# mLSTM core: value products with the tokens on the partitions, a column of ones, statistics as columns, a ring of seven weight tiles

## What is computed

```python
inter = bt + m[..., None]
mt = jnp.maximum(inter, dmat.max(-1))
w_inter = jnp.exp(inter - mt)
sqk = jnp.einsum('bhtd,bhsd->bhts', qt, kt) * jnp.exp(dmat - mt[..., None])
num = (w_inter[..., None] * jnp.einsum('bhtk,bhkv->bhtv', qt, c_mat)
       + jnp.einsum('bhts,bhsv->bhtv', sqk, vt))
den = w_inter * jnp.einsum('bhtk,bhk->bht', qt, n_vec) + sqk.sum(-1)
ht = num / jnp.maximum(jnp.abs(den), jnp.exp(-mt))[..., None]
...
h = h_fwd + h_bwd
```

## Time and profile before

| | us |
|---|---|
| median of 3 runs | 4366.0 |
| lowest, highest | 4365.65, 4366.83 |
| the profiled execution, its own time | 4371.4 |
| span of its trace | 4369.6 |
| PE busy in the span | 3929.4 (90%) |
| DVE busy | 2095.5 (48%) |
| ACT busy | 1521.8 (35%) |

### The profile page before, as it was taken

One profiled execution on the slowest core, in us unless ns is written; L12 is line 12 of the kernel. 1 busy time (PEld: TensorE's weight loads), 2 busy tenths in 40 slices (PEclk: granted clock), 3 DMA queues, 4 the chain that ended last, 5 costly groups with the idle time before them and its releaser, 6 DMA issues. The chain is left out here.

```text
span 4369.6 us, 51714 instructions
## 1 busy us (share of the span) xinstructions
PE 3929.4 (90%) x20400; PEld 2995.5 (69%) x20400; DVE 2095.5 (48%) x3118; ACT 1521.8 (35%) x2347; POOL 400.0 (9%) x354
## 2 busy tenths in 40 slices
PE   7888778879999998889789999999988799999998
PEld 5456667668878776566567878876656577777876
DVE  4867464574343335536546443333544635543332
ACT  4444312533332224314444332233313534333232
POOL 0024322000011112010000001100000000001100
PEclk9899778979999998889999999999989999999999
DMA  3011001203322222011112322222101022332222
GB/s 109 10 51 44 1 2 51 67 10 112 93 86 96 84 86 66 29 44 43 67 48 82 95 91 92 95 80 79 49 29 58 1 102 74 93 94 87 94 79 73
DMA packets 83486, 289.30 MB, mean 66 GB/s; under 512 B 9168, under 2 KB 9296, under 8 KB 82000
## 3 DMA queue, kind: packets, MB, share of 16 engines
q1 hardware_dynamic: 83136, 286.30, 20.4%
q10 hardware_dynamic: 144, 0.15, 0.0%
HBM read 284.32 MB, written 2.10 MB: 66 GB/s over the span
## 5 line engine op out<-in xcount | busy, mean ns | idle before, releaser
L547 DVE TENSOR_TENSOR weights_lo_r<-raw_weights,weights_hi_r 128x1024 fp32r<-128x1024 f32 (+2 forms) x554 | 633.1, 1143 | 1752.3 <-ACT weights_hi_r L541 1752.2
L541 ACT ACTIVATE weights_hi_r<-raw_weights 128x1024 fp32r<-128x1024 f32 (+2 forms) x554 | 547.5, 988 | 1865.2 <-PE ps L614 1829.4
L613 PE MATMUL ps<-xn_r,weights_hi_r 128*128 128x512 f32 x2816 | 1117.2, 397 | 0.0
L612 PE MATMUL ps<-xn_hi,weights_hi_r 128*128 128x512 f32 x1952 | 805.1, 412 | 84.4 <-DVE xn_r L607 27.1
L614 PE MATMUL ps<-xn_hi,weights_lo_r 128*128 128x512 f32 x1952 | 777.9, 399 | 0.0
L613 PEld LDWEIGHTS ps<-xn_r,weights_hi_r 128*128 128x128 f32 x2816 | 539.9, 192 | 126.9 <-issue 10.6
L612 PEld LDWEIGHTS ps<-xn_hi,weights_hi_r 128*128 128x128 f32 x1952 | 377.2, 193 | 203.7 <-issue 93.8
L614 PEld LDWEIGHTS ps<-xn_hi,weights_lo_r 128*128 128x128 f32 x1952 | 376.7, 193 | 83.0
L612 PE MATMUL ps<-y_r,weights_hi_r 128*128 128x512 f32 x1056 | 421.3, 399 | 1.6 <-PEq L858 1.6
L614 PE MATMUL ps<-y_r,weights_lo_r 128*128 128x512 f32 x1056 | 421.0, 399 | 0.0
L612 PE MATMUL ps<-hidden_hi,weights_hi_r 128*128 128x512 f32 x528 | 215.9, 409 | 31.9 <-DVE hidden_r L607 31.9
(11 more groups left out here) (490 smaller groups left out, 5521.2 us busy)
## 6 DMA issues: line engine op xcount, KB each, us to landing
raw_weights<-in_w_ffn_dram SPq DMA_DIRECT2D x132, 512.0 KB, 3.7
raw_weights<-in_w_down_dram SPq DMA_DIRECT2D x48, 512.0 KB, 3.5
raw_weights<-in_w_out_dram SPq DMA_DIRECT2D x24, 512.0 KB, 3.5
bias_table<-in_window_bias_dram SPq DMA_DIRECT2D x8, 1280.0 KB, 10.5
raw_weights<-in_w_down_dram SPq DMA_DIRECT2D x24, 384.0 KB, 3.1
raw_weights<-in_w_hgrn_dram SPq DMA_DIRECT2D x16, 512.0 KB, 3.4
raw_weights<-in_w_mix_ssm_dram SPq DMA_DIRECT2D x16, 512.0 KB, 3.7
raw_weights<-in_w_a_qk_dram SPq DMA_DIRECT2D x16, 512.0 KB, 3.5
```

Source lines behind the costliest of these rows:

```text
L541: act.activation(self.k.w_hi[:, g % 2, 0:chunk.width], self.k.raw[:, slot, 0:chunk.width], ACT.Copy)\
L547: dve.tensor_tensor(self.k.w_lo[:, g % 2, 0:chunk.width], self.k.raw[:, slot, 0:chunk.width], self.k.w_hi[:, g % 2, 0:chunk.width].bitcast ...
L612: pe.matmul(out, w_hi, x_hi, start=start, stop=False)
L613: pe.matmul(out, w_hi, x_lo, start=False, stop=False)
```

## The change

Only the core block and what prepares it change.

- **Value products turned round.** `dist` blocks of 128 keys x 128 queries become the stationary operand, and the moving operand is the v tile with the tokens on the partitions and a 129th column of ones (`v_one`, 128 x 4 x 4 x 129; GpSimd sets the ones). One product of 129 columns gives the values and, in the last column, the sum of weights, with queries on the partitions. A step has 4, 3, 2 or 1 such products, a unit 10. The all-ones product is gone.
- **Statistics as columns.** The preparation transposes the m rows too (8 more small transposes), ACT takes exp(-m) of a 128x32 tile (`floor_cols`), and the spread of the floor row is gone. `finish` does the maxima and the reciprocal on 128x4 tiles. The forward unit's values are scaled by ACT in 4 activations of 128x128 (`scale_first`) into `tap`; the backward unit's are scaled and added by DVE in 4 instructions of 128x128.
- **Turning back.** PE transposes the head's sum (4 transposes of 128x128, `turn`) into bank 6, and ACT copies it to `y` (`take`).
- **Ring of seven, one step later.** `dist` has 7 buffers, and the weights overwrite it, so `prob` is gone. PE calls `weigh(s - 2)` and DVE `weight(s - 2)`; `finish` moves behind the fourth step of a unit. Before its bound, DVE waits only that the ring's buffer is free. The spread into bank u % 2 waits for the bounds of the unit two before, no longer for its end.

The diff, cut to its core:

```diff
@@ project @@
-            width = tokens[1].shape[2]
+            width = int(np.prod(tokens[1].shape[2:]))
...
-                    act.activation(tokens[1][:, j, :], k.ps[:, (t0 + j) % 4, 0:width], ACT.Copy).then_inc(tokens_used, 1)
+                    o, taken = tokens[1][:, j], k.ps[:, (t0 + j) % 4, 0:width]
+                    if len(o.shape) == 3:
+                        taken = taken.rearrange("p (h v) -> p h v", h=o.shape[1])
+                    act.activation(o, taken, ACT.Copy).then_inc(tokens_used, 1)
...
@@ MlstmPreparation @@
+        pool.memset(self.one_col, 1.0).then_inc(self.edges, 1)
...
-                mm = pe.transpose(self.cols[:, j, r, :], self.g_[:, r, j * P:(j + 1) * P],
-                                  k.const("ident", H)[:, 0:H])
+                for to, rows in ((self.cols, self.g_), (self.m_cols, self.m_)):
+                    mm = pe.transpose(to[:, j, r, :], rows[:, r, j * P:(j + 1) * P], k.const("ident", H)[:, 0:H])
...
-        act.wait_ge(self.rows_ready, 10)
-        act.activation(m_[:, :, :], m_[:, :, :], ACT.Exp, scale=-1.0).then_inc(self.m_ready, 1)
         act.wait_ge(self.cols_turned, 1)
+        act.activation(self.m_col[:, :, :, :], self.m_cols, ACT.Exp, scale=-1.0).then_inc(self.m_ready, 1)
         act.activation(self.g_col[:, :, :, :], self.cols, ACT.Copy).then_inc(self.cols_ready, 1)
...
@@ mlstm_branch @@
-        v_tok = sb("v_tok", [P, NT, A_WIDTH])
+        v_one = sb("v_tok", [P, NT, H, P + 1])
...
+            RING = 7
+            dist = raw[:, :, :].rearrange("p a b -> p (a b)")[:, 0:RING * T].rearrange("p (a t) -> p a t", a=RING)
...
+            def values(u, i):
+                return k.ps[:, 4 + 2 * (u % 2) + i // 2, (i % 2) * (P + 1):(i % 2) * (P + 1) + P + 1]
             @block.tensor
             def _(pe):
...
                     u, back, h, j, ts = place(s)
                     pe.wait_ge(prob_ready, s + 1)
                     if s % NT == 0 and u >= 2:
-                        pe.wait_ge(h_ready, u - 1)
-                    pr = prob[:, s % 2, ts]
-                    pe.matmul(k.ps[:, 4 + u % 2, ts], v_tok[:, j, h * P:(h + 1) * P], pr, start=(s % NT == 0),
-                              stop=(s % NT == NT - 1))
-                    pe.matmul(k.ps[:, 6 + u % 2, ts], k.const("ones"), pr, start=(s % NT == 0),
-                              stop=(s % NT == NT - 1)).then_inc(pv_done, 1)
-                    if s % NT == NT - 1:
-                        pe.wait_ge(bounded, s + 1)
-                        pe.matmul(bank(k.ps, u % 2), k.const("ident", H)[:, h:h + 1].broadcast_to([H, P]),
-                                  m_[:, back, :], start=True, stop=True).then_inc(floor_spread, 1)
+                        if back:
+                            pe.wait_ge(y_ready, h)
+                        else:
+                            pe.wait_ge(first_half, NT * h)
+                    for i in range(0, j + 1) if back else range(j, NT):
+                        mm = pe.matmul(values(u, i), dist[:, s % RING, i * P:(i + 1) * P], v_one[:, j, h, :],
+                                       start=(s % NT == 0 and i % 2 == 0), stop=(j == (0 if back else i)),
+                                       skip_group_check=True)
+                    mm.then_inc(pv_done, 1)
+                def turn(h):
+                    pe.wait_ge(both_halves, NT * (h + 1))
+                    for i in range(NT):
+                        mm = pe.transpose(k.ps[:, 6, i * P:(i + 1) * P], tap[:, h % 2, i * P:(i + 1) * P],
+                                          k.const("ident"))
+                    mm.then_inc(turned, 1)
                 for s in range(STEPS):
                     u, back, h, j, ts = place(s)
                     if s % NT == 0:
                         if u >= 2:
-                            pe.wait_ge(h_ready, u - 1)
+                            pe.wait_ge(bounded, NT * (u - 1))
                         pe.matmul(bank(k.ps, u % 2), k.const("ident", H)[:, h:h + 1].broadcast_to([H, P]),
                                   M_[:, back, :], start=True, stop=True).then_inc(spread, 1)
                     if s >= 2:
                         pe.wait_ge(prob_ready, s - 1)
                     pe.matmul(k.ps[:, 2 + s % 2, ts], qk[:, H + h, j * P:(j + 1) * P], qk[:, h, ts],
                               start=True, stop=True).then_inc(qk_done, 1)
-                    if s:
-                        weigh(s - 1)
+                    if s >= 2:
+                        weigh(s - 2)
+                    if s % NT == 0 and u >= 3 and back:
+                        turn(h - 1)
+                weigh(STEPS - 2)
                 weigh(STEPS - 1)
+                turn(H - 1)
             @block.gpsimd
             def _(pool):
                 for s in range(STEPS):
                     u, back, h, j, ts = place(s)
                     pool.wait_ge(exped, s + 1)
-                    d = dist[:, s % 2, j * P:(j + 1) * P]
+                    d = dist[:, s % RING, j * P:(j + 1) * P]
                     pool.tensor_tensor(d, d, k.const("ge" if back else "le"), ALU.mult).then_inc(masked, 1)
             @block.scalar
             def _(act):
-                def absolute(u):
-                    act.wait_ge(pv_done, NT * (u + 1))
-                    act.activation(den[:, u % 2, :], bank(k.ps, 6 + u % 2), ACT.Abs).then_inc(den_ready, 1)
+                def scale_first(u):
+                    h = u // 2
+                    act.wait_ge(scale_step, 3 * u + 3)
+                    if h >= 2:
+                        act.wait_ge(turned, h - 1)
+                    for i in range(NT):
+                        act.activation(tap[:, h % 2, i * P:(i + 1) * P], values(u, i)[:, 0:P], ACT.Copy,
+                                       scale=stat[:, u % 2, i:i + 1]).then_inc(first_half, 1)
+                def take(h):
+                    act.wait_ge(turned, h + 1)
+                    act.activation(y[:, h, :], bank(k.ps, 6), ACT.Copy).then_inc(y_ready, 1)
                 for s in range(STEPS):
                     u, back, h, j, ts = place(s)
                     act.wait_ge(bounded, s + 1)
-                    act.activation(dist[:, s % 2, ts], dist[:, s % 2, ts], ACT.Exp, scale=-1.0).then_inc(exped, 1)
-                    if s % NT == 2 and u:
-                        absolute(u - 1)
-                absolute(UNITS - 1)
+                    act.activation(dist[:, s % RING, ts], dist[:, s % RING, ts], ACT.Exp, scale=-1.0).then_inc(exped, 1)
+                    if s % NT == 3 and u and back:
+                        scale_first(u - 1)
+                    if s % NT == 0 and u >= 3 and back:
+                        take(h - 1)
+                take(H - 1)
             @block.vector
             def _(dve):
                 def weight(s):
                     u, back, h, j, ts = place(s)
+                    d = dist[:, s % RING, ts]
                     dve.wait_ge(masked, s + 1)
                     dve.wait_ge(qk_done, s + 1)
-                    if s >= 2:
-                        dve.wait_ge(pv_done, s - 1)
-                    dve.tensor_tensor(prob[:, s % 2, ts], dist[:, s % 2, ts], k.ps[:, 2 + s % 2, ts], ALU.mult)\
-                        .then_inc(prob_ready, 1)
+                    dve.tensor_tensor(d, d, k.ps[:, 2 + s % 2, ts], ALU.mult).then_inc(prob_ready, 1)
                 def finish(u):
-                    back, h, d = u % 2, u // 2, den[:, u % 2, :]
-                    dve.wait_ge(den_ready, u + 1)
-                    dve.wait_ge(floor_spread, u + 1)
-                    dve.tensor_tensor(d, d, bank(k.ps, u % 2), ALU.max).then_inc(den_step, 1)
-                    dve.wait_ge(den_step, 3 * u + 1)
-                    dve.reciprocal(d, d).then_inc(den_step, 1)
-                    dve.wait_ge(den_step, 3 * u + 2)
+                    back, h, r = u % 2, u // 2, stat[:, u % 2, :]
+                    sums = k.ps[:, 4 + 2 * (u % 2):6 + 2 * (u % 2), P:2 * P + 2:P + 1]
+                    pairs = lambda ap: ap.rearrange("p (a b) -> p a b", a=2)
+                    dve.wait_ge(pv_done, NT * (u + 1))
+                    dve.scalar_tensor_tensor(out=pairs(r), in0=sums, scalar=-1.0, in1=pairs(m_col[:, :, back, h]),
+                                             op0=ALU.mult, op1=ALU.max).then_inc(scale_step, 1)
+                    dve.wait_ge(scale_step, 3 * u + 1)
+                    dve.tensor_tensor(pairs(r), sums, pairs(r), ALU.max).then_inc(scale_step, 1)
+                    dve.wait_ge(scale_step, 3 * u + 2)
+                    dve.reciprocal(r, r).then_inc(scale_step, 1)
                     if back:
-                        dve.tensor_tensor(d, d, bank(k.ps, 4 + u % 2), ALU.mult).then_inc(den_step, 1)
-                        dve.wait_ge(den_step, 3 * u + 3)
-                        dve.tensor_tensor(y[:, h, :], y[:, h, :], d, ALU.add).then_inc(h_ready, 1)
-                    else:
```

(54 more changed lines are left out.)

2 lines of the change are left out of this document (1 added, 1 removed).

## The result

| | median us | lowest to highest | runs |
|---|---|---|---|
| before | 4365.8 | 4360.3 to 4366.8 | 4 |
| changed | 4269.6 | 4268.3 to 4270.8 | 4 |

The ratio is 0.9779, 95% interval 0.9766 to 0.9792: 96 us less. The forecast was 4266.6. The profiled execution of the changed kernel takes 4268.3, against 4371.4 before: 103.1 less.

The account below looks back on a forecast made before the run. The core was taken as a PE-DVE loop at two buffers' lead, PE paying for its gaps in clock. Gains of 107.3 - 6 - 1.9 = 99.4 us took 4371.4 to 4272.0, less 5.4 for the median: 4266.6, range 4240 to 4300.

Parts of the forecast that it names:

- The sum: Whole kernel: 107.3 gained in the cores, minus 6 for clock and 1.9 for transposes, gives 99.4 us less.
- Plain boundary 6.9 us, turning boundary 7.6: Core, between units: four boundaries of 6.9 us with PE idling 1.2 before q.k, three of 7.6 where a head turns back.
- the turning chain: Where a head is turned back: `take` waits for transposes, then second step's exp, mask and weight follow; P at 7.6 us.
- Value products at 0.118 us with their loads hidden: PE in the core: 20 instructions a unit step at 0.118 us at the full clock, 2.36 us in all.
- Rival 3: Value products' weight loads stand bare, adding 3.8 us a unit, 61 in all: 4328; chance 0.05.
- The small operations at 0.18 us each, the four scalings at 1.1: DVE's `finish`: three 128x4 operations, together 0.54 us, and the backward unit's four 128x128 instructions, 1.1 in all.
- Start 6.6, end 4.9 us: Core's ends: 6.6 us until unit 0's fourth q.k product, 4.9 from the last such product to the end of `take`.
- Clock: Core: one more halved stretch of 7 us a layer, costing 3 us each, 6 in all; mean clock 0.9 or more.
- Restart of the next projection: Behind the core: PE's gap shrinks from 5.95 to about 3 us; gain left at nought, range 0 to 4 us.
- Rival 1: Core is PE-bound with a shorter boundary wait, a unit costing PE's 5.9 us: 4242; chance 0.12.
- Rivals 4 and 5: Slower through exposed value products, 4464, chance 0.04; no measurable change because the gain returns behind the core, chance 0.02.
- Rival 2: Clock stays down for half of the core, 14.6 us more a layer instead of 3: 4290; chance 0.18.

Follow-up runs that it names:

- third version: Changed kernel with DVE's weight ahead of the bound at a unit's start, spread before the fourth q.k product, `take` one step later: 4233.1 us, again 4236.0.

## Why the prediction was right, step by step

- **The sum, and some luck.** On the profiled execution the forecast was 4272.0 and 4268.3 was measured, 3.7 lower: the cores gained 102.9 us where 107.3 - 6 = 101.3 were laid out, and the 1.9 us for the eight more transposes a layer don't show (the changed profile is 0.9 and 0.5 us longer ahead of the two cores and 1.6 shorter behind them, less than such stretches differ between profiles of one kernel). For the median the forecast then took off 5.4 us, because the profile before lay that far above its median; the profile of the changed kernel lies 1.3 us below its median. The two misses, 3.7 and 6.7 us, have opposite signs and leave the 3 us between 4266.6 and 4269.6. That closeness is luck; the layout of the cores is not.
- **Plain boundary 6.9 us, turning boundary 7.6.** Measured 6.88 and 7.61. The wait of 1.2 us in front of q.k is 1.17, released by DVE's weight, and the turning chain (transposes L2942, `take` L2986, exp, mask, weight) shows as laid out; POOL's mask releases the weight, and that the fourth q.k product:

```profile
1811.76 0.60 PE L2942 MATMUL ps<-consts,tap 128*128 128x128 f32 x4
...
1812.39 0.60 ACT L2986 ACTIVATE y<-ps 128x512 f32<-128x512 f32 x1 [1.76 <-PE ps L2942]
...
1812.89 1.02 ACT L2991 ACTIVATE qk_raw<-qk_raw 128x384 f32<-128x384 f32 x3
...
1813.97 0.56 DVE L3005 TENSOR_TENSOR qk_raw<-qk_raw,ps 128x384 f32<-128x384 f32 x1 [1.44 <-POOL qk_raw L2971]
...
1814.58 0.49 PE L2955 MATMUL ps<-qk 128*128 128x128 f32 x2
```

- **Value products at 0.118 us with their loads hidden.** Measured 0.11. Rival 3, bare loads, is out. The Trainium skill, page "TensorE: Matmul & The Clock Gate", Part 3, Packing small matmuls, has the rule by which a load overlaps running matmuls only in other row groups; loads of all 128 rows overlap here, so the trace does not bear it out. The same part also lets a load go ahead into a background weight buffer. With that the measured step agrees, though no run shows the buffer itself.
- **The small operations at 0.18 us each, the four scalings at 1.1.** Measured 0.19, 0.19, 0.22 from start to start, and 1.13; ACT's four take 1.14, 0.29 each and just under the 0.3 to 0.58 laid out. All lie beside PE's work.
- **Start 6.6, end 4.9 us.** The fourth q.k product starts 5.6 us after the first spread in the first core and 7.1 in the second, 6.4 in the mean (the first spread takes 1.30 and 1.47 us, against 2.04 in the earlier trace rows, so the clock rose earlier), and in the first core, from the last fourth q.k product, 1845.23, to the end of `take` at 1850.18 pass 4.95.
- **Clock.** One halved stretch of 7 us a core, at a price of 3 us, was allowed on top of the slow start. Behind the first unit the first core has one unit with a halved piece (8.55 us for 6.88, a price of 1.7), the second two (8.57 and 8.54, 3.4 in all). With the start, at a mean of 0.94 the first core spent 12% of 62.8 us, 7.5, on the lower level, the second at 0.89 22%, 14.5; the 0.9 or more that the prediction wanted to see was just missed there. Cores of 64.9 us were forecast, 62.5 and 65.8 measured (without the 0.3 us to the next block).
- **Restart of the next projection.** It begins halved as before, although PE now idles 0.94 us in front of it and not 5.95. The prediction put that gap at about 3 us; leaving the gain at nought was right:

```profile
1850.48 0.77 PE L612 MATMUL ps<-xn_hi,weights_hi_r 128*128 128x512 f32 x1 [0.94 <-PEq L2899]
...
1851.05 0.63 PE L613 MATMUL ps<-xn_r,weights_hi_r 128*128 128x512 f32 x1
```

- **What the prediction did not see.** It counted PE's saved columns and DVE's saved stall into one layout and never asked what either is worth alone. The runs did: the stall alone is worth 36 us a core, the all-ones products alone nothing or a little less than nothing, and the last 12 to 14 us come only with the rest of the change, the longer lead among it. The ring's depth stood in the text only as cover, the order at the boundary as a wait to be taken as it is; they turned out to be worth 50 to 55 and 7 to 14 us a core.
- **Rival 1** (PE-bound, 4242) is out for this kernel: the wait stands. Its reading of the cause was right, though. With the order changed at both places (third version) PE is busy without a gap, a unit costs 5.64 or 6.08 us, near the 5.9 counted for PE's work, and the kernel takes 4233 to 4236.
- **Rivals 4 and 5** (slower, or the gain returns behind the core) are out: the step is 0.11 us, and 102.9 of the 103.1 us are gained in the cores.
- **Rival 2** (clock down for half of the core) is out for this kernel, but it is the mechanism of every run that was slower than laid out: the ring of three, the reciprocal put back, the all-ones products left out.

## What to carry to other kernels

Where PE waits for another engine in a loop, shorten the other engine's longest instruction first, and give the loop one more step of lead. Here, taking work off PE while that wait stood only made PE idle longer and lowered its clock. Lay one period of the loop end to end from rows of the trace and look for an instruction that stands behind one whose input comes late: moving it in front of that one cost nothing here and gave 7 and 9 us of blocks of 63 and 66 us. Before sizing a ring, ask which engine's step each wait points to: one buffer too few turned overlap into taking turns.

## What the runs showed of the hardware

- Removing 64 of 224 PE instructions from a core left PE as long busy as before (95.15 against 93.42 us), because the mean granted clock fell from 0.81 to 0.62.
- With waits of about 1 us in front of every step (ring of three, units of 13 to 16 us, so 3 to 4 us a step) the clock was at the lower level for most of the core (a mean of 0.63). With one wait of 1.17 us in 6.9 us the mean was 0.89 to 0.94, and nearly without waits 0.92 to 0.98. The share of waiting alone doesn't order these: with every q.k product doubled the same 1.16 us stood in 9.03 us, and twice as many units (10 of 14) fell below the full clock.
- A float32 product of 128 or 129 columns with a 128-column load of its own costs 0.11 to 0.12 us an instruction at the full clock, next to the 0.11 that 128 columns of a 512-column product take (0.86 us in two instructions). So the load costs next to nothing beside it.
- The same code ahead of the first core took between 1772 and 1788 us in the profiles of the changed kernel and its variants. The same kernel alone differs: 1787.7 and 1780.3 for the changed one, 1772.1 and 1782.0 for the third version. So differences under some 15 us between kernels measured at different times say nothing without the windows.
